# The latents' gated scan: blocks of 128 tokens with scores at three levels and one state a head, in place of chunks of 32 with eight states

## The reference

```python
def chunked_gated_linear_scan(q, k, v, log_f, s0):
    # S_t = diag(f_t) S_{t-1} + k_t^T v_t ; o_t = S_t^T q_t, in chunks of 32
    b = cumsum(log_f in the chunk); b_last = b[..., -1:, :]
    q_dec, k_inv = q * exp(b), k * exp(-b)
    scores = where(causal in the chunk, q_dec @ k_inv^T, 0);  o_intra = scores @ v
    kv_chunk = (k * exp(b_last - b))^T @ v;  decay = exp(b_last)
    # step over chunks: S <- decay * S + kv_chunk, from s0; s_starts = S before each
    return o_intra + q_dec @ s_starts
```

## Time and profile before

| | us |
|---|---|
| median of 3 runs | 2768.81 (2767.35 to 2769.12) |
| profiled execution, time | 2770.57 |
| profiled execution, span | 2768.8 |
| TensorE busy | 2693.5 |
| VectorE busy | 1838.5 |
| ACT busy | 1260.5 |
| GpSimd busy | 59.0 |

### The profile page before, as it was taken

One profiled execution on the slowest core, in us unless ns is written; L12 is line 12 of the kernel. 1 busy time (PEld: TensorE's weight loads), 2 busy tenths in 40 slices (PEclk: granted clock), 3 DMA queues, 4 the chain that ended last, 5 costly groups with the idle time before them and its releaser, 6 DMA issues.

```text
span 2768.8 us, 34200 instructions
## 1 busy us (share of the span) xinstructions
PE 2693.5 (97%) x13574; PEld 2262.1 (82%) x13574; DVE 1838.5 (66%) x2461; ACT 1260.5 (46%) x1646; POOL 59.0 (2%) x80
## 2 busy tenths in 40 slices
PE   7999999999999999999999999999889999999999
PEld 6899889878888888888788788777668888888887
DVE  5657756576888888766866675766656666554555
ACT  3433555455434435454645455444344444434433
POOL 0000000000000000000000000111000000000000
PEclk9989999999999999999999999999989999999999
DMA  6767555467778787866676654444347777566555
GB/s 217 244 220 240 185 181 175 160 214 258 257 252 260 249 265 252 278 210 205 205 230 214 214 176 145 148 131 131 117 142 244 250 245 241 178 195 190 189 192 174
DMA packets 303312, 572.51 MB, mean 207 GB/s; under 512 B 20429, under 2 KB 30049, under 8 KB 303025
## 3 DMA queue, kind: packets, MB, share of 16 engines
q1 hardware_dynamic: 299712, 559.77, 62.3%
q0 software_dynamic: 3264, 10.49, 1.4%
q10 hardware_dynamic: 176, 0.07, 0.0%
HBM read 568.16 MB, written 2.10 MB: 206 GB/s over the span
## 4 chain that ended last, share of the span: by engine, by line
PE 87%; DVE 5%; ACT 3%; DMA 2%; issue 2%; SPq 0%; DVEq 0%; ACTq 0%
PE ps L1636 24%; PE ps L1638 24%; PE ps L1637 24%; PE ps L1630 2%; PE ps L1632 2%; PE ps L1631 2%; DMA raw<-in_w_in 2%; PE ps L1591 2%; DVE wlo L2176 1%; ACT whi L1893 1%; PE ps L1819 1%; PE ps L1648 1%; PE ps L1701 1%; PE ps L1671 1%; DVE acc L2194 1%
## 5 line engine op out<-in xcount | busy, mean ns | idle before, releaser
L2176 DVE TENSOR_TENSOR wlo<-raw,whi 128x1024 fp32r<-128x1024 f32 x857 | 1043.4, 1224 | 697.6 <-ACT whi L1893 689.8
L1893 ACT ACTIVATE whi<-raw 128x1024 fp32r<-128x1024 f32 x857 | 900.1, 1056 | 1039.7 <-PE ps L1638 297.1
L1636 PE MATMUL ps<-whi,th 128*128 128x512 f32 (+2 forms) x3168 | 1257.6, 397 | 32.3 <-DVE wlo L2176 19.0
L1638 PE MATMUL ps<-whi,tl 128*128 128x512 f32 (+2 forms) x3168 | 1234.6, 390 | 0.0
L1637 PE MATMUL ps<-wlo,th 128*128 128x512 f32 (+2 forms) x3168 | 1233.5, 389 | 0.0
L1636 PEld LDWEIGHTS ps<-whi,th 128*128 128x128 f32 x3168 | 602.9, 190 | 157.4 <-DVE wlo L2176 23.4
L1638 PEld LDWEIGHTS ps<-whi,tl 128*128 128x128 f32 x3168 | 603.2, 190 | 125.2
L1637 PEld LDWEIGHTS ps<-wlo,th 128*128 128x128 f32 x3168 | 603.8, 191 | 118.1 <-issue 1.9
L2194 DVE SCALAR_TENSOR_TENSOR acc<-raw,silc,acc 128x512 f32<-128x512 f32 x480 | 344.3, 747 | 58.1 <-DMA raw<-in_w_mod 53.2
L1630 PE MATMUL ps<-th,whi 128*128 128x256 f32 x640 | 188.0, 294 | 4.1 <-DVE wlo L2176 4.1
L1631 PE MATMUL ps<-th,wlo 128*128 128x256 f32 x640 | 183.3, 286 | 0.0
(11 more groups left out here) (275 smaller groups left out, 1354.6 us busy)
## 6 DMA issues: line engine op xcount, KB each, us to landing
raw<-in_w_in SPq DMA_DIRECT2D x240, 512.0 KB, 4.0
raw<-in_w_down SPq DMA_DIRECT2D x216, 512.0 KB, 4.7
raw<-in_w_mod SPq DMA_DIRECT2D x192, 512.0 KB, 3.7
raw<-in_w_gate_up SPq DMA_DIRECT2D x176, 512.0 KB, 3.5
raw<-in_w_up SPq DMA_DIRECT2D x128, 512.0 KB, 3.9
raw<-in_w_out SPq DMA_DIRECT2D x64, 512.0 KB, 3.7
raw<-in_xattn_wkv SPq DMA_DIRECT2D x16, 512.0 KB, 3.6
raw<-in_xattn_wq SPq DMA_DIRECT2D x8, 512.0 KB, 3.5
```

What stands on the lines that cost most here:

```text
L1636: pe.matmul(p, xh, wh[:, c, c0:n], start=a and (form == "rows" or tb == 0), stop=False, skip_group_check=True)
L1638: ins = pe.matmul(p, xl, wh[:, c, c0:n], start=False, stop=z, skip_group_check=True)
L1893: self.e.activation(t.his[g % NHI][:, 0:n], t.raws[j % NRAW][:, 0:n], ACT.Copy).then_inc(*s.hi.up(g))
L2176: self.e.tensor_tensor(t.los[j % NRAW][:, 0:n], t.raws[j % NRAW][:, 0:n], t.his[g % NHI][:, 0:n].bitcast(F), ALU.subtract).then_inc(*s.lo. ...
```

## The change

The scores reach over the whole block of 128 now, and one state a head, at the border of the two blocks, is left. Where query and key lie in one chunk of 32, E2 and E1 are multiplied as before. For two chunks of one pair the key side is multiplied by its chunk's decay first (K1). For the halves of the block both sides carry the decays of the chunks between (K2, Q2). These products overwrite their 32 x 32 and 64 x 64 parts of the full score product. Q3 is E1 times the decays back to the block's start; it reads the first state S0 in one block and the new state S1 = decay * S0 + update in the other. `dec` gets 12 columns a block: one, four chunk decays, products of two, three and four of them, one. The two masks of 32-wide chunks for the gate's sums go; the gate is summed over a block of 128, and only over the one that the update needs. `head_masked`, its tiles and its small constant load go. Cut to its core:

```diff
 def forget(...)
-        for tb in range(2):
+        for tb in [d] if latent else range(2):
             bank = self.big.take()
             self.forget_b(key, tb, d, latent, bank)
-        self.forget_c(key)
+        self.forget_c(key, slice(d, d + 1) if latent else slice(0, 2))
 # states(u), outputs(u)
-                    up = [self.big.take(), self.big.take()]
-                    sc = self.big.take()
-                    self.head_states(u, up, sc)
+                    bank = self.big.take()
+                    self.head_states(u, bank)
+                    u["E1"].give((s.hs, u["k"]), (s.hq3, u["k"]))
-                    for z in ("ST", "HS", "E1"):
+                    for z in ("ST", "HS"):
                         u[z].give((s.ho, u["k"]))
-                        masked(U[i])
 # TensorE, head_states (e is the bank's tile)
-        for tb in range(2):
-            pe.matmul(up[tb].tile[:, :], t.hE[:, tb, hs], u["vm"][tb].tile[:, :, :], ...)
+        pe.matmul(e[:, 256:384], t.hE[:, d, hs], t.hV[u["g"]][:, d, hs], ...)      # update
...
         for tb in range(2):                                                        # as before
+            pe.matmul(e[:, at:at + 128], E2[:, at:at + 128], E1[:, at:at + 128], ...)
+        self.wait_ge(*s.hk1.at(u["k"]))
+        for tb in range(2):
+            for i in range(2):
+                kc, qc = 2 * i + d, 2 * i + 1 - d
+                at = 128 * tb + 32 * qc
+                pe.matmul(e[32 * kc:32 * kc + 32, at:at + 32], K1[:, 2 * tb + i, :], E1[:, at:at + 32], ...)
+        self.wait_ge(*s.hk2.at(u["k"]))
+        self.wait_ge(*s.hq2.at(u["k"]))
+        for tb in range(2):
+            at = 128 * tb + 64 * (1 - d)
+            ins = pe.matmul(e[64 * d:64 * d + 64, at:at + 64], K2[:, tb, :, :], Q2[:, tb, :, :], ...)
 # TensorE, head_outputs
-        self.wait_ge(*s.hc.at((u["k"], 6)))
-        for c in range(8):
-            ins = pe.matmul(e[rows, at:at + 128], u["E1"].tile[:, 32 * c:32 * c + 32], u["HS"].tile[:, c, :], ...)
+        self.wait_ge(*s.hq3.at(u["k"]))
+        pe.matmul(e[:, 128 * d:128 * d + 128], Q3[:, d, :, :], t.S0[:, 8 * d + 4 * u["g"] + h, :], ...)
+        self.wait_ge(*s.hc.at(u["k"]))
+        pe.matmul(e[:, 128 - 128 * d:256 - 128 * d], Q3[:, 1 - d, :, :], S1[:, :], ...)
 # VectorE, head_turned: after dec copy (h3), E2 *= k (h4), a product of decays (hp), E1 *= q (h5)
+        dv.tensor_tensor(K1, E2 of every second chunk, its decay, ALU.mult)             # hk1
+        dv.tensor_tensor(F2[:, :, 3:10:6], ..., ALU.mult)                               # ht, decays
+        dv.tensor_tensor(K2, half of E2, decays, ALU.mult)                              # hk2
+        dv.tensor_tensor(Q2, half of E1, decays, ALU.mult)                              # hq2
+        dv.tensor_tensor(Q3, E1, decays, ALU.mult)                                      # hq3
 # VectorE, head_states: the scores' mask (hw) as before, with the block's triangle
-        dv.tensor_copy(HS[:, order[0], :], t.S0[:, 8 * d + 4 * g + h, :])
-        for i, (c, nx) in enumerate(zip(order[:7], order[1:])):
-            dv.scalar_tensor_tensor(out=HS[:, nx, :], in0=HS[:, c, :], scalar=dd[:, c:c + 1], in1=up[tb]..., ...)
+        dv.scalar_tensor_tensor(out=S1, in0=t.S0[:, 8 * d + 4 * g + h, :], scalar=t.dec[...], in1=e[:, 256:384], ...)
```

More of the change, by code:

```diff
@@ L50, in constants @@
     same = (i // 32) == (j // 32)
-    for k, m in enumerate(((i <= j) & same, (i >= j) & same, (i > j) & same, (i < j) & same, i > j, i < j)):
+    for k, m in enumerate(((i <= j) & same, (i >= j) & same, i <= j, i >= j, i > j, i < j)):
         c[:, HGM + 128 * k:HGM + 128 * k + 128] = m
-    c[:, HGM + 768:HGM + 772] = (i // 32) == np.arange(4)[None, :]
     return c
@@ L1397, in value @@
             self.gemm(op1, w2, 0, 3072 + 512 * g, 512, range(16), self.rows(f"hv{g}", t.hV[g], 0, 512, 0, ACT.Copy, used=ends + fin))
[L1400 to L1403, removed]
+        self.e1s, self.e2s, self.sts, self.hss = Ring(t.hE1), Ring(t.hE2), Ring(t.hST), Ring(t.hS)
+        self.hss.after = [list(scrL) for _ in t.hS]
+        self.g_after, self.lb_after, self.o_after, self.free_e = scrL, scrL, scrL, scrL
+        self.scan_ones()
         gate = lambda g, d: self.gemm(op1, w2, 0, 1024 + 1024 * d + 512 * g, 512, range(16), self.lat_gate(g, d))
@@ L1779, in forget_b @@
         self.wait_all(bank.after)
[L1780 to L1786, removed]
+        far = not latent and tb == d
+        ins = pe.matmul(bank.tile[:, :], t.hgm[:, 4 + d, :], t.hA[:, tb, :], start=True, stop=not far, skip_group_check=True)
+        if far:
+            ins = pe.matmul(bank.tile[:, :], t.ones[:, :], t.hA[:, 1 - tb, :], start=False, stop=True, skip_group_check=True)
         ins.then_inc(*s.f5.up((key, tb)))
@@ L1810, in head_turned, with head_states @@
         ins.then_inc(*s.h0.up(u["k"]))
-    def head_states(self, u, up, sc):
-        t, s, pe, h = self.t, self.s, self.e, u["h"]
+    def head_states(self, u, bank):
+        t, s, pe, h, d, e = self.t, self.s, self.e, u["h"], u["d"], bank.tile
+        E1, E2, (_, K1, K2, Q2, _) = u["E1"].tile, u["E2"].tile, u["HS"].tile
         hs = slice(128 * h, 128 * h + 128)
         self.wait_ge(*s.f7.at(u["key"]))
[L1816 to L1820, removed]
+        self.wait_all(bank.after)
+        pe.matmul(e[:, 256:384], t.hE[:, d, hs], t.hV[u["g"]][:, d, hs], start=True, stop=True, skip_group_check=True).then_inc(
+            *s.hu.up(u["k"]))
@@ L1821, in head_states @@
         self.wait_ge(*s.h4.at(u["k"]))
         self.wait_ge(*s.h5.at(u["k"]))
-        self.wait_all(sc.after)
         for tb in range(2):
-            ins = pe.matmul(sc.tile[:, 128 * tb:128 * tb + 128], u["E2"].tile[:, 128 * tb:128 * tb + 128],
-                            u["E1"].tile[:, 128 * tb:128 * tb + 128], start=True, stop=True, skip_group_check=True)
+            at = 128 * tb
+            pe.matmul(e[:, at:at + 128], E2[:, at:at + 128], E1[:, at:at + 128], start=True, stop=True, skip_group_check=True)
@@ L1836, in head_outputs @@
                       skip_group_check=True)
-        self.wait_ge(*s.hc.at((u["k"], 6)))
-        for c in range(8):
[L1839 to L1842, removed]
+        self.wait_ge(*s.hq3.at(u["k"]))
+        self.wait_ge(*s.z9.at(("ctx", u["g"], d)))
+        pe.matmul(e[:, 128 * d:128 * d + 128], Q3[:, d, :, :], t.S0[:, 8 * d + 4 * u["g"] + h, :], start=False, stop=True,
+                  skip_group_check=True)
+        self.wait_ge(*s.hc.at(u["k"]))
+        pe.matmul(e[:, 128 - 128 * d:256 - 128 * d], Q3[:, 1 - d, :, :], S1[:, :], start=False, stop=True,
+                  skip_group_check=True).then_inc(*s.ho.up(u["k"]))
     def read_turn(self, key, slot, bank, op):
@@ L2422, in gate_keys, with forget_c, scan_ones, head_turned @@
         dv.tensor_scalar(t.hK[:, :, :], t.hA[:, :, :], -1.0, 1.0, ALU.mult, ALU.add).then_inc(*s.f3.up(key))
-    def forget_c(self, key):
+    def forget_c(self, key, tbs):
         t, s = self.t, self.s
-        for tb in range(2):
+        for tb in range(tbs.start, tbs.stop):
             self.wait_ge(*s.f6.at((key, tb)))
         self.wait_ge(*s.f3.at(key))
[L2429 to L2433, removed]
+        self.e.tensor_tensor(t.hE[:, tbs, :], t.hE[:, tbs, :], t.hK[:, tbs, :], ALU.mult).then_inc(*s.f7.up(key))
+    def scan_ones(self):
+        t, s = self.t, self.s
+        for i, col in enumerate((0, 11)):
+            self.e.tensor_copy(t.dec[:, :, col], t.ones[:, 0:4]).then_inc(*s.h_one.up(i))
+    def head_turned(self, u, bank):
+        t, s, dv, k, h, d = self.t, self.s, self.e, u["k"], u["h"], u["d"]
+        E1, E2, (_, K1, K2, Q2, Q3) = u["E1"].tile, u["E2"].tile, u["HS"].tile
+        F2 = t.dec[:, 2 * (h % 2):2 * (h % 2) + 2, :]
+        chunks = lambda z: z[:, :].rearrange("p (b c t) -> p b c t", b=2, t=32)
+        wide = lambda f: f.unsqueeze(3).broadcast_to([128, 2, f.shape[2], 32])
         self.wait_ge(*s.h1.at(k))
-        self.wait_all(dec)
-        dv.tensor_copy(dd, E1[:, :].rearrange("p (c t) -> p c t", t=32)[:, :, 31 if u["d"] == 0 else 0]).then_inc(*s.h3.up(k))
+        dv.tensor_copy(F2[:, :, 1:11:3], chunks(E1)[:, :, :, 31 if d == 0 else 0]).then_inc(*s.h3.up(k))
         self.wait_ge(*s.h2.at(k))
@@ new lines, in head_turned @@
+        dv.tensor_tensor(K2[:, :, :, :], chunks(E2)[:, :, 2 * d:2 * d + 2, :], wide(F2[:, :, 2:5:2] if d == 0 else F2[:, :, 7:10:2]),
+                         ALU.mult).then_inc(*s.hk2.up(k))
+        self.wait_ge(*s.h_one.at(1))
+        self.wait_ge(*s.h5.at(k))
+        dv.tensor_tensor(Q2[:, :, :, :], chunks(E1)[:, :, 2 - 2 * d:4 - 2 * d, :], wide(F2[:, :, 0:8:7] if d == 0 else F2[:, :, 4:12:7]),
+                         ALU.mult).then_inc(*s.hq2.up(k))
+        self.wait_ge(*s.ht.at(k))
@@ L2446, in head_states @@
+        dv.tensor_tensor(Q3[:, :, :, :], chunks(E1), wide(F2[:, :, 0:4] if d == 0 else F2[:, :, 8:12]), ALU.mult).then_inc(*s.hq3.up(k))
+    def head_states(self, u, bank):
```

(23 more changed lines are left out.)

74 lines of the change are left out of this document (35 added, 39 removed).

## The result

The changed kernel takes 2744.59 us (2742.11 to 2748.84, 4 runs) against 2768.08 (4 runs) before, a ratio of 0.9918 with an interval of 0.9905 to 0.9931. A second measurement on another occasion gave 0.9919 (0.9905 to 0.9932). In microseconds the two ratios are a gain of 22.7 and 22.4, with intervals from 19 to 26; the medians of the first differ by 23.5. The forecast was a gain of 19.2, at the low end of that interval, and a time of 2749.6.

A forecast was written before the change was run, and what follows sets the result against it. TensorE bounds the kernel, busy 97% of the span. Savings of 29.9, 3.4 (gate) and 0.3 (last scan's end) less 14.4 for small products give 19.2 us: 2768.8 becomes 2749.6, stated range 2741 to 2761.

The forecast's parts named there:

- The update: TensorE's state update per head: two 128 x 128 instructions, 0.22 us, replace four of 512 columns; saves 24.0 us in all.
- the outputs: TensorE's new output per head: eight 128 x 128 instructions in one tile shape, 0.89 us, replacing L1835 and L1840's 1.11.
- no wait for hS: TensorE's wait at L1840 for the seven-step chain on hS goes, saving 1.2 us (between 0.7 and 1.7).
- The gate's 3.4: Gate sums (L1781) for one block instead of two: 0.86 us saved a key, four keys, 3.4 us.
- The block: Added TensorE work: twelve instructions of 32 x 32 and 64 x 64 products, 0.9 us a head, 14.4 us in all.
- the three changes of shape: Tile-shape changes around and inside the small products on TensorE: 0.09 us in, 0.2 between, 0.2 out, each head.
- (a): Small products dearer, weight load and matmul in series: 1.36 to 1.8 us a head, 2757 to 2764 us; chance 0.15.
- (b): Small products cheaper: 0.43 us a head, gain 26.7 us, 2742 us; chance 0.08.
- (c): Each small instruction ends before the next begins: 3.8 us a head, 27 us slower, 2796 us; chance 0.05.
- The cover of the waits: VectorE finishes K1 at least 1.3 us and Q2 1.1 us before TensorE needs them, so no new waits.
- The end of the last scan: hO no longer waits behind hS: 0.6 us gained, 0.3 of it new; TensorE's 5.7 us idle at the readout stays.
- The 3 us set aside for such shifts: Shifting later stretches that run at 1.2 GHz moves the forecast or any rival by some 3 us.

The follow-up runs named there:

- its own experiment: Changed kernel with the gate's sums, exponential and product with k made for both blocks of 128 again: ratio 0.9930 to the kernel before, 3.3 us above the changed kernel.
- the run with seven steps: Kernel before with the state update made for one masked chunk a block (128 columns, not 512), all seven hS steps kept: ratio 0.9958, 11.5 us.
- with one step: Kernel before with the state update cut to 128 columns and one step on hS in place of seven: ratio 0.9929, 19.5 us.

## Why the prediction was right

- **TensorE's occupancy sets the time.** Shown: what is added to it returns in full (9.6 to 12.0 us of the stretch for 16 x 0.62, 5.9 for 16 x 0.36, 0.86 a key for the gate's 0.86), and 0.9 us a head on VectorE returns nothing.
- **What goes.** The update 0.22, the outputs 0.89, no wait for hS: as forecast. The gate's 3.4 is shown by its own experiment.
- **What comes.** The block: 0.83 measured, 0.9 forecast. The term that was mis-sized is the pace of the 32-wide instructions, 15 ns and not 27; the 64-wide ones are 60 and not 54. The twelve cost 0.36 and not 0.44, which leaves 0.47 for the three changes of shape, forecast at 0.49. So the block's sum came out for the reasons given, although the price of the 64-wide ones and of the middle change had no row of their own and were read from neighbours. A part of a change's price lies where I had not looked for it, 0.11 of it in the sums behind the block. Rivals (a), (b) and (c), at 1.36, 0.43 and 3.8 us, are all excluded.
- **VectorE.** 4.6 us a tick against 4.7. I expected it idle longer than 1.3 before the masked scores; it is 1.25 there, and 0.59 in front of the decays' copy.
- **The cover of the waits.** Forecast 1.3 at least for K1 and 1.1 for Q2; five extra products, 2.3 us, leave TensorE waiting 0.7 + 0.25 us at a first head, so the cover there was some 1.6 us for K1 and 1.3 for Q2.
- **The end of the last scan.** TensorE's idle time before the last transposes fell from 5.72 to 5.05; I had kept it at 5.7 and put 0.3 down for the split that no longer stands ahead of hO. With the chain kept (the run with seven steps) it was 5.70, with one step 5.07, so the chain is the cause.
- **The size.** At like clock the stretch lost 21.4 us, 2.2 more than the sum of 19.2. The block gives 16 x 0.07 = 1.1 of it, the end of the scan 0.4; the rest, 0.7, I can't assign. The first profile's 25.0 us between spans holds 2.3 more for one stall behind which the clock did not fall. The 3 us set aside for such shifts were of the right size.

## What to carry to other kernels

Where TensorE is busy through a stage, price a change in starts per instruction, read from the nearest rows, and price each change of tile shape as its own item: here two of them (0.26 us) cost as much as eight or nine of the twelve small instructions (0.36 us). Work out first how much of a saving the next engine would let through: here dropping TensorE's columns alone gave 11.5 us and dropping VectorE's chain with them 19.5. To compare two profiles within a few microseconds, compare like stretches and look at the granted clock behind each stall before a difference is given to the change.

## What was not expected of the hardware

- Behind the same stall of 3.7 us the clock fell to 1.2 GHz in two executions and not in a third, one of the same program: 2.3 us. Of the other nine profiles, three had it fallen in the same way and six for a part of the time (0.72 in 6 us); none stayed at full clock.
- A change of tile shape costs little ahead of a long product (0.10 us before 512 columns) and more ahead of short ones (some 0.2 behind the small block, half of it in the sums that follow; 0.22 + 0.08 behind the eight state readings).
- VectorE's copy of the first state (L2453, 128 x 128) lasted 0.22 us where GpSimd was idle and 0.52 beside GpSimd's masking products; in the run with seven steps on fewer columns it lasted 1.1 at two heads, and in the one with one step 0.92 to 0.96 at nine, all beside them. At the eight first heads of those two runs' keys it lasted 0.22 at the point where one masking product ended and the next began. VectorE's other operations of that tick did not stretch. What the removed masking products were worth was not tested by itself:

```profile
1748.86 2.18 POOL L1582 TENSOR_TENSOR hM<-hV,chm 128x512 f32<-128x512 f32 x2 [3.44 <-PE ps L1819]
...
1750.02 1.10 DVE L2453 COPY hS<-S 128x128 f32<-128x128 f32 x1
```
